# Two transformer blocks with routed experts: tokens and sums are turned before their norms, one more place for weights, a branch moved

## What is computed

```python
def reference(x, mem, ...):
    z = rms_norm(x, norm_mix) @ w_in          # u, v, q, k, val: tokens of x
    ... gated unit, differential attention, x = x + mixed
    x = x + memory_attention(rms_norm(x, norm_xq), rms_norm(mem, norm_mem), ...)
    x = x + hierarchical_moe(rms_norm(x, norm_ffn), ...)   # silu(t @ gate[e]) * (t @ up[e]) @ down[e]
    x = rms_norm(x, norm_final)
    q, k, v = split(rms_norm_2(x, norm_mix_pre_2) @ attn_w_qkv_2)
    ... x = x + rms_norm_2(attention @ w_o, norm_mix_post_2)
    return x + rms_norm_2(square(relu(rms_norm_2(x, norm_ffn_pre_2) @ w_up_2)) @ w_down_2, norm_ffn_post_2)

def rms_norm(x, g): return x * rsqrt(mean(x * x) + 1e-6) * g
```

## Time and profile before

| | us |
|---|---|
| runs shown: median (lowest to highest) | 1015.07 (1014.17 to 1015.34) |
| the profiled execution's own time | 1013.95 |
| its span in the trace | 1012.7 |
| TensorE busy | 956.6 |
| VectorE busy | 441.1 |
| ScalarE busy | 360.3 |
| DMA: 289.66 MB, mean GB/s | 286 |

### The profile page before, as it was taken

How to read it: one execution, slowest core, us unless ns; L and a number is a source line. 1 busy time by engine, 2 the same in 40 slices (tenths; PEclk the granted TensorE clock), 3 DMA queues, 4 the chain that set the end, 5 groups by cost and what they waited for, 6 DMA issues and landing times.

```text
span 1012.7 us, 13539 instructions
## 1 busy us (share of the span) xinstructions
PE 956.6 (94%) x5353; PEld 653.8 (65%) x5353; DVE 441.1 (44%) x757; ACT 360.3 (36%) x593; POOL 26.2 (3%) x40
## 2 busy tenths in 40 slices
PE   6999989998999999999999999985999989999997
PEld 5979878985444444444444444332998879998886
DVE  5856555445232232222222222214564755555434
ACT  7635446433121121111111112114455544554332
POOL 1400000000000000000000000000000000000000
PEclk9989999998999999999999999999999989999999
DMA  9943443486899999999999999999645535555501
GB/s 319 361 146 126 167 164 134 161 316 264 311 430 421 429 428 426 427 429 428 429 428 430 428 428 428 428 428 362 212 156 165 167 107 164 180 192 172 205 1 42
DMA packets 72629, 289.66 MB, mean 286 GB/s; under 512 B 4993, under 2 KB 44545, under 8 KB 60546
## 3 DMA queue, kind: packets, MB, share of 16 engines
q1 hardware_dynamic: 72002, 288.79, 73.8%
q10 hardware_dynamic: 576, 0.17, 0.1%
HBM read 287.90 MB, written 1.05 MB: 285 GB/s over the span
## 4 chain that ended last, share of the span: by engine, by line
PE 79%; issue 6%; ACT 6%; DVE 5%; DMA 4%; POOL 1%; SPq 0%; ACTq 0%; DVEq 0%
PE bank L1519 21%; PE bank L433 11%; PE bank L434 11%; PE bank L435 11%; PE bank L1541 10%; PE bank L1493 4%; DMA ring<-in_w_up 3%; ACT w_high L494 3%; PE bank L1552 3%; DVE w_low L523 1%; DVE arena L2303 1%; PE bank L1530 1%; ACT hidden_high L2127 1%; PE bank L723 1%; PE bank L761 1%
## 5 line engine op out<-in xcount | busy, mean ns | idle before, releaser
L1519 PE MATMUL bank<-ring,arena 128*64 128x512 f32 x1024 | 228.7, 598 | 7.9 <-issue 7.1
L523 DVE TENSOR_TENSOR w_low<-ring,w_high 128x2048 fp32r<-128x2048 f32 x76 | 174.1, 2290 | 122.3 <-ACT w_high L494 122.3
L494 ACT ACTIVATE w_high<-ring 128x2048 fp32r<-128x2048 f32 x76 | 145.1, 1909 | 120.8 <-PE bank L435 120.7
L1519 PEld LDWEIGHTS bank<-ring,arena 128*64 128x64 f32 x1024 | 75.5, 137 | 140.9 <-issue 139.0
L1541 PE MATMUL bank<-ring,arena 128*64 128x512 f32 x512 | 116.9, 597 | 5.3 <-issue 5.3
L433 PE MATMUL bank<-xT_high,w_high 128*128 128x256 f32 x384 | 112.0, 292 | 2.6 <-DVE xT_low L532 1.8
L434 PE MATMUL bank<-xT_low,w_high 128*128 128x256 f32 x384 | 109.8, 286 | 0.0
L435 PE MATMUL bank<-xT_high,w_low 128*128 128x256 f32 x384 | 109.7, 286 | 0.0
L1644 DVE SCALAR_TENSOR_TENSOR y_low<-bank,arena,y_high 64x512 fp32r<-64x512 f32 x64 | 48.0, 750 | 139.3 <-ACT y_high L1584 138.8
L1584 ACT ACTIVATE y_high<-bank,arena 64x512 fp32r<-64x512 f32 x64 | 43.7, 683 | 135.3 <-PE bank L1541 134.9
L1571 ACT ACTIVATE arena<-bank 128x256 f32<-128x256 f32 x32 | 12.3, 385 | 191.1 <-PE bank L1519 191.1
(11 more groups left out here) (280 smaller groups left out, 1455.9 us busy)
## 6 DMA issues: line engine op xcount, KB each, us to landing
ring<-in_w_down SPq DMA_DIRECT2D x32, 2048.0 KB, 25.0
ring<-in_w_gate SPq DMA_DIRECT2D x31, 2048.0 KB, 21.3
ring<-in_w_up SPq DMA_DIRECT2D x31, 2048.0 KB, 25.8
ring<-in_w_up SPq DMA_DIRECT2D x16, 1024.0 KB, 5.6
ring<-in_w_down SPq DMA_DIRECT2D x16, 1024.0 KB, 5.0
ring<-in_attn_w_qkv SPq DMA_DIRECT2D x12, 1024.0 KB, 11.8
ring<-in_w_in SPq DMA_DIRECT2D x10, 1024.0 KB, 11.7
ring<-in_w_kv_mem SPq DMA_DIRECT2D x8, 1024.0 KB, 5.2
```

The lines of the kernel that those rows point to most:

```text
L494: SC.activation(parts[buffer[0][u]][0][:, :], lanes[n % len(lanes)], ACT.Copy).then_inc(*high.inc(u))
L523: DVE.tensor_tensor(p[1][:, :], lanes[n % len(lanes)], p[0][:, :].bitcast(F32), ALU.subtract).then_inc(*split.inc(u))
L1519: last = PE.matmul(GU[t * SLOTS:(t + 1) * SLOTS, 0:NGU], xs[:, k, :], wgu[:, :, k, t * (DE // JT):(t + 1) * (DE // JT)], start=k == 0, sto ...
```

## The change

- **Tokens raw.** x's rows are transposed as loaded. Square, mean and power of x follow beside products. The norm of each token is put on the products: a row of norms, made wide (`widen`), turned ("rh") and copied, multiplies the banks of u, q and k when VectorE evacuates them (`features_out`); v and val take it as a scale per partition. u's Gelu runs on the evacuated values. mem is loaded behind u0 and turned behind u1.
- **Sums raw.** The four banks of the experts' sums are copied as they are and transposed; the gain column is norm_mix_pre times norm_final, and the norms of q, k, v are put on their products as above ("r1"). The product with the row norm_final, its squares and the means follow behind. norm_final's row is loaded behind the last experts' weights.
- **Places.** `extra` is a tenth piece; `bc` lies in it. Expert 3's down weights use it, and the places of experts from 4 on move up by one (`places_of`), with new waits in `early_loads`. The second block's lanes and parts are set to match.
- **Branch.** The last pair's scatter stands behind the branch, with a signal of its own after the first 128 tokens.
- **Constant products.** `keep_busy`: 8 products of ones into bank 7 before x's transposes, 6 behind them.
- The scratch area for dynamic DMA is set to 2048 bytes.

```diff
-hT00 hT01 hT10 hT11 +v.0 +v.1 -v.0 -v.1 u0@2 memT00@6 memT01@7 memT10@0 memT11@1 u1@3 q0@4 sguw@5 k0@2 +O0@6 +O1@7
+hT00 hT01 hT10 hT11 +v.0 +v.1 -v.0 -v.1 u0@2 rh@6 u1@3 memT00@6 memT01@7 memT10@0 memT11@1 q0@4 sguw@5 k0@2 +O0@6 +O1@7
...
-    bc = nc.alloc_sbuf_tensor("gain_rows", [P, 1024], F32)
...
+    extra = nc.alloc_sbuf_tensor("extra_piece", [P, PIECE], F32)
+    bc = extra[:, 0:1024]
...
-    lanes1, parts1 = pieces(*LANE_SLOTS), weight_parts("w1", slot_at(3))
+    lanes1, parts1 = pieces(*LANE_SLOTS), weight_parts("w1", slot_at(3), slot_at(3) + 2 * TILE)
...
-    lanes2, parts2 = pieces(3, 4, 5, 6), weight_parts("w2", slot_at(0))
+    lanes2, parts2 = pieces(3, 4, 5, 6), weight_parts("w2", slot_at(1), slot_at(0))
...
+    def keep_busy(bank, n):
+
+        for _ in range(n):
+            PE.matmul(bank[:, 0:P], ones[:, :], ones[:, :], start=True, stop=True, skip_group_check=True)
...
-        for u in order1[0:2]:
+        for u in order1[0:3]:
             load_first(u)
         for h in range(NH):
             SP.dma_start(memX[:, h, :], a["mem"][0, h * P:(h + 1) * P, :]).then_inc(*loads.inc(f"mem{h}"))
-        for u in order1[2:4]:
-            load_first(u)
+        load_first(order1[3])
...
-        load_row("norm_final", a["norm_final"].rearrange("(l n) -> l n", l=1))
+        SP.dma_start(gains[:, G_FINAL, :], a["norm_final_column"]).then_inc(*loads.inc("gain_final"))
...
+        PE.wait_ge(*consts.at("ones"))
+        keep_busy(banks[7], 8)
         PE.wait_ge(*consts.at("ident"))
-        turn(bank1, "hT", [(rows_v.at(f"h{h}"), rows_s.at(f"h{h}")) for h in range(NH)])
+        turn(bank1, "hT", [(loads.after(f"x{h}", 1),) for h in range(NH)], src=X)
+        keep_busy(banks[7], 6)
...
+        bank = open_bank(bank1, "rh")
+        for h in range(NH):
+            PE.wait_ge(*norm_wide.at(f"h{h}"))
+            last = PE.transpose(bank[:, h * P:(h + 1) * P], wide_h[:, h * P:(h + 1) * P], ident[:, :])
+        last.then_inc(*turned.inc("rh"))
+        f("u1", hT)
...
+        def u_gelus(u, t):
+            SC.wait_ge(*bank1.freed(u))
+            SC.activation(t, t, ACT.Gelu).then_inc(*u_gelu.inc(u))
...
-        for h in range(NH):
-            SC.wait_ge(*loads.after(f"x{h}", 1))
-            square_sum(X[:, h, :], XN[:, h, :], f"h{h}", stat("h", h))
-        for h in range(NH):
-            scale_half("h", h, XN, X)
...
+        high("u1")
         for h in range(NH):
             scale_half("mem", h, memX, memX)
-        SC.wait_ge(*early1.at("v.1"))
-        evacuate(bank1, "v.0", v[:, 0, :], func=ACT.Gelu)
-        SC.wait_ge(*unit1.at("v.1"))
-        evacuate(bank1, "v.1", v[:, 1, :], func=ACT.Gelu)
-        high("u1")
-        feature_out("u0", flat(uT[:, 0:2, :]), func=ACT.Gelu)
+        for h, whole in ((0, early1), (1, unit1)):
...
+            SC.wait_ge(*whole.at("v.1"))
+            SC.wait_ge(*rstd.at(f"h{h}"))
+            evacuate(bank1, f"v.{h}", v[:, h, :], stat("h", h), ACT.Gelu)
         high("q0")
+        SC.wait_ge(*turned.at("rh"))
+        evacuate_part(bank1, "rh", row_h)
+        u_gelus("u0", flat(uT[:, 0:2, :]))
+        high("k0")
+        u_gelus("u1", flat(uT[:, 2:4, :]))
         SC.wait_ge(*loads.after("gain_mem", 1))
+        turned_highs(bank1, "memT", 1, memT[0], G_MEM)
...
+        def features_out(u, dst, scale):
+
+            DVE.wait_ge(*unit1.at(u))
+            DVE.wait_ge(*bank1.freed("rh"))
+            DVE.scalar_tensor_tensor(out=dst, in0=banks[bank1.bank[u]][:, :].rearrange("p (n t) -> p n t", t=S),
+                                     scalar=scale, in1=row_h.rearrange("p (n t) -> p n t", n=1).to_broadcast([P, 2, S]),
+                                     op0=ALU.mult, op1=ALU.mult).then_inc(*bank1.inc(u))
...
+        features_out("u0", uT[:, 0:2, :], 1.0)
...
         low("q0")
-        turned_lows(bank1, "memT", 0, memT, G_MEM)
+        features_out("u1", uT[:, 2:4, :], 1.0)
+        low("k0")
...
+        features_out("q0", qT[:, 0:2, :], float(DQK) ** -0.5)
+        low("val.0")
+        features_out("k0", kT[:, 0:2, :], 1.0)
...
+        features_out("q1", qT[:, 2:4, :], float(DQK) ** -0.5)
         low("km0")
+        features_out("k1", kT[:, 2:4, :], 1.0)
...
-    def gate_up(q, n, w, buffer, e, chunks_=range(KC)):
+    def gate_up(q, n, gate, up, buffer, e, chunks_=range(KC)):
         xs = XTE[buffer][:, :, e * SLOTS:(e + 1) * SLOTS]
-        wgu = ring[:, w * PIECE:(w + 2) * PIECE].rearrange("p (m c n) -> p m c n", m=2, c=KC)
+        wgu = ring[:, :].rearrange("p (s c n) -> p s c n", s=RING, c=KC)[:, gate:up + 1:up - gate, :, :]
...
+        if mark:
+            last.then_inc(mark, 1)
...
+    def expert_loads(q, n, n0):
+
+        gate, up, dn = places_of(n0)
+        SP.wait_ge(*q.at("gate_up", n - 2))
+        if up < gate + 2:
+            load_piece(gate, expert_of(w_gate, n), place_sem[gate])
+            load_piece(up, expert_of(w_up, n), place_sem[up])
+        else:
+            load_piece(up, expert_of(w_up, n), place_sem[up])
+            load_piece(gate, expert_of(w_gate, n), place_sem[gate])
+        SP.wait_ge(*q.at("down", n - 2))
+        load_piece(dn, expert_of(w_down, n), place_sem[dn])
+
+    EXTRA = RING
+
+    def places_of(n):
+
+
+        if n < 4:
+            w = (6 + 3 * n) % RING
+            return w, w + 1, EXTRA if n == 3 else w + 2
+        w = (5 + 3 * n) % RING
+        return (1, w, 0) if w + 1 == RING else (w, w + 1, w + 2)
...
+        elif n == 3:
+            for part in range(4):
+                if part < 3:
+                    SP.wait_ge(quarters, part + 1)
+                else:
+                    SP.wait_ge(*q.at("gate_up", 1))
                 o = slice(part * PIECE // 4, (part + 1) * PIECE // 4)
-                SP.dma_start(ring[:, (w + i) * PIECE:(w + i + 1) * PIECE][:, o], src[3][:, o]).then_inc(slot_sem[w + i], 16)
-        SP.wait_ge(*q.at("down", 1))
-        SP.dma_start(ring[:, (w + 2) * PIECE:(w + 3) * PIECE], w_down[3]).then_inc(slot_sem[w + 2], 16)
+                SP.dma_start(piece(gate)[:, o], w_gate[n][:, o]).then_inc(place_sem[gate], 16)
+                SP.dma_start(piece(up)[:, o], w_up[n][:, o]).then_inc(place_sem[up], 16)
+            SP.wait_ge(*vgain.at(1))
+            load_piece(dn, w_down[n], place_sem[dn])
...
+            first, second = ((gate, w_gate), (up, w_up)) if gate < up < gate + 2 else ((up, w_up), (gate, w_gate))
+            SP.wait_ge(*q.at("down", n - 3))
+            load_piece(first[0], first[1][n], place_sem[first[0]])
+            SP.wait_ge(*q.at("gate_up", n - 2))
+            load_piece(second[0], second[1][n], place_sem[second[0]])
+            load_piece(dn, w_down[n], place_sem[dn])
...
-    for u in order2[0:6]:
+    for u in order2[0:4]:
         load_second(u)
     SP.wait_ge(*q.at("gate_up", NE - 1))
+    for u in order2[4:6]:
+        load_second(u)
+    load_row("norm_final", a["norm_final"].rearrange("(l n) -> l n", l=1))
...
-    scatter(q, NE, NE, LAST % 3, 0, False)
-    scatter(q, NE, NE, LAST % 3, 1, True)
...
+    tokens0_scattered = nc.alloc_semaphore("tokens0_scattered")
+    scatter(q, NE, NE, LAST % 3, 0, False, tokens0_scattered)
+    scatter(q, NE, NE, LAST % 3, 1, True)
...
-        turn(bank2, "pT", [(rows_v.at(f"p{h}"),) for h in range(NH)])
+                PE.wait_ge(*norm_wide.at(f"{r}{h}"))
+                last = PE.transpose(bank[:, h * P:(h + 1) * P], wide[r][:, h * P:(h + 1) * P], ident[:, :])
+            last.then_inc(*turned.inc(r))
+
+        for h in range(NH):
+            turn_sum("pT", h, XN, [bank2.freed(f"z{2 * h + j}") for j in range(2)], "pT")
...
+        turn_norms("r1")
...
+        def z_copy(b):
+            evacuate(bank2, f"z{b}", XN[:, b // 2, 512 * (b % 2):512 * (b % 2 + 1)])
...
-        part_squares("z", 0, ["z0", "z1"])
-        part_square("z", 1, 0, "z2")
-        z_squares(0)
-        part_square("z", 1, 1, "z3")
-        z_squares(1)
-        turned_highs(bank2, "pT", 0, xT2[0], G_PRE2)
-        turned_highs(bank2, "pT", 1, xT2[0], G_PRE2)
+        z_copy(3)
+        SC.wait_ge(*z_gained.at("columns"))
+        for c4 in range(2):
+            for h in range(NH):
+                turned_highs(bank2, "pT", h, xT2[0], G_PRE2, groups=(c4,))
+        for h in range(NH):
+            SC.wait_ge(*bank2.freed(f"z{2 * h}"))
+            SC.wait_ge(*bank2.freed(f"z{2 * h + 1}"))
+            z_squares("zr", h, XN, arena[3], small[:, 16 + 2 * h:17 + 2 * h])
...
+        SC.wait_ge(*z_gained.at(0))
+        z_squares("z", 0, X, arena[4], small[:, 20:21])
+        high("q0")
+        SC.wait_ge(*z_gained.at(1))
+        z_squares("z", 1, X, arena[4], small[:, 21:22])
...
+        norm_row("r1")
...
+        def z_gain(h):
+            for b in (2 * h, 2 * h + 1):
+                DVE.wait_ge(*bank2.freed(f"z{b}"))
+            DVE.tensor_tensor(X[:, h, :], XN[:, h, :], bc[:, :], ALU.mult).then_inc(*z_gained.inc(h))
...
+        DVE.wait_ge(*loads.after("gain_final", 1))
```

(24 more changed lines are left out.)

276 lines of the change are left out of this document (147 added, 129 removed).

## The result

| | before | changed |
|---|---|---|
| median, lowest to highest, us | 1015.21, 1014.17 to 1016.53 | 1006.61, 1005.58 to 1008.21 |
| the profiled execution, us | 1013.95 | 1006.05 |
| its span | 1012.7 | 1004.8 |

The ratio is 0.991 (95% interval 0.9893 to 0.9926): faster by 8.6 us, forecast 8.5. The sum was right; its first term had the wrong sign in the traces, and the two others were off by about 1 us each. I read the start of the same products in both traces; the stretches add up to each trace's last product.

What follows compares the result with a forecast made beforehand. TensorE works almost everywhere, so only its gaps can be won; the DMA's stream sets the expert stage's end. Gains 1.7 + 2.8 + 4.0 = 8.5 take the profiled 1013.95 to 1005.4; median forecast 1006.6, range 1001.5 to 1012.0.

Steps and rivals of the forecast that it cites:

- first term: First block to its first scores: turning tokens raw gains 1.7 us, bounds 0 and 2.9.
- the two stalls I priced: First block: TensorE loses 0.8 us waiting for q0; k0's evacuation queues behind low val.0, first scores near 48.9.
- The term of 1.7: First block to its first scores: gain from tokens turned raw, 1.7 us, bounds 0 and 2.9.
- size 2.8: Expert stage: the extra piece for weights lets loads start earlier, a lead of 2.8 us, bounds 2.0 and 4.1.
- the dry second at 272: Expert stage: the DMA moved nothing from 272 to 273 before; with the earlier issues it never runs dry there.
- 5.0 for 4.0: Between experts and second block: raw sums and the moved branch gain 4.0 us, bounds 2.0 and 6.4.
- the 6.4: Between the blocks: first product at 704.1 instead of 710.54, saving 6.4 us before deductions for clock and branch.
- The deduction of 2.1 for the clock: Between the blocks: half clock on products loses up to 3.4 us, 1.6 if in the scatter; 2.1 taken.
- The branch's 0.3: Branch moved ahead of the last scatter, under a 3.0 us wait: cost between 0 and 0.9, 0.3 taken.
- The rival of a fetch behind the branch: Branch ahead of the last scatter: the jump outlasts its wait, scatter up to 2.4 us late, 1009.0; chance 0.07.
- cost 0: Feature units' evacuations moved from ScalarE to VectorE: 8.2 us of VectorE beside a full TensorE, cost 0.
- The slow side: Rival: moved evacuations delay the lows behind them, 3.0 us for each of twelve, 18 if half, 1024.6; chance 0.05.

Runs made afterwards that it cites:

- a1: The changed kernel without its two groups of constant products (8 and 6) at the start: median 1007.72 us, ratio 0.992 to the kernel before.
- a3: The changed kernel with the last pair's scatter ahead of the branch over the spill code again, sums still raw: 1008.92 us, ratio 0.9935.
- b1: The kernel before with k3 moved to bank 6, a2 to 7 and a3 to 1 in the second attention: 1013.37 us, ratio 0.9974.
- c1: The changed kernel with nine constant products behind the last down product, ahead of the branch, in TensorE's wait for the last y: 1008.77 us, ratio 0.9921.
- c2: The changed kernel with six constant products in TensorE's wait for the chosen experts and three ahead of the first gather: 1003.80 us, ratio 0.9874.
- d0: The changed kernel itself, unaltered, measured again: 1005.74 us, ratio 0.9897 to the kernel before.
- e3: The kernel with waits filled before the experts and at the second attention's end, but loads of experts 3 to 6 at before's events: 1002.76 us, ratio 0.9865.
- c3: The changed kernel with five constant products ahead of turning the second attention's sums and six behind it: 1004.32 us, ratio 0.9877.
- e2: The kernel with waits filled before the experts and at the second attention's end, the gating's second-half products moved behind val.1: 1003.27 us, ratio 0.9867.

## Why the prediction was right, and where it was not

**First block: wrong.** The step to the first product held: 10.05 against 9.75, v.0's first high at 8.55 against 8.4; the 1.35 us from there were 1.5. The first constant products took 3.78 us for the 2 I gave them, being at half rate; that cost nothing, since without them (a1) the transposes start at 4.82 instead of 4.79. Of the two stalls I priced, low q0's was 1.31 for 0.8 (0.42 in a3), first scores 49.33 for 48.9. What failed is that the sum ends at the first scores: it has no term from there to the experts. Two things took 2.1 us. One is the same queue of VectorE I had watched at q0, further on: k1's evacuation stands behind low km0, and the fifth scores wait for it, 1.56 us instead of the 0.88 in the kernel before (0.7 us):
```profile
87.97 0.49 PE L691 MATMUL bank<-arena 64*128 64x128 f32 x4 [1.56 <-DVE arena L1134]
```
The other is the clock, which I followed only between the blocks. Most of the gating and the products behind it run at half:
```profile
62.00:66.00 4.00, 4.00 (x11) 2.91 (x12) 2.83 (x2) 0.46 (x1) 0.00 (x0) 0.50 0.10 16
66.00:70.00 4.00, 4.00 (x11) 3.04 (x11) 1.98 (x3) 0.80 (x2) 0.00 (x0) 0.50 0.60 246
```
for 10.2 us here and 6.8 before (62 to 69), 1.5 us more. The comparison with b1 above gives the same split, 0.6 and 1.5. In seven other executions with the new first block it is 6.8, and 3.4 more at 131 to 137, 10.2 again; c1 and c2 have 10.2 and 3.4. The first gather came at 243.64 and 243.60 in two executions of before's first block, at 243.87 to 244.65 in the eight of the new one with 10.2 us at half. The term of 1.7 was -0.95 in the pair of traces and -0.3 to -1.0 over these executions, below its lower bound of 0. But the third execution of before's block, b1, had its first gather at 247.38, by its half-rate start (1.8 us) and 3.4 us more at half clock. Against it the new block gains 2.7 to 3.5 us. So the failed term is shown for the traces compared; what it is on average needs more executions of the kernel before. b1 has 3.4 us at 135 to 140 as well, so the second fall isn't the new block's alone; why it came in the other two not at all is open.

**Experts' stream: mechanism right, size 2.8 for about 2.** Every issue came in the predicted order and spacing, the dry second at 272 went, waits of 4.7 us for the 5.1 forecast. That last agreement is partly luck. The waits were 7.2 us in a1 and 3.6 in d0 with the new events. The changed kernel's clock was at half for 3.4 us at 667 to 671, and its last wait for weights, 1.4 us near 683 (the 1.39 of the earlier trace rows), is missing. In all 14 traces one goes with the other: where the clock falls at some point from 664 to 672 us (eight) that wait is absent, where it doesn't (six) it is there, 1.4 us. TensorE works longer and the weights catch up, so a fall there costs next to nothing. The waits fell by 3.2 us and the stretch to the last gate-up by only 1.9 (446.5 to 444.6), since the other 1.3 went into that slower work. The one pair of traces can't give the lead more closely: the stage varies by 3.3 us.

**Between the blocks: right in kind, 5.0 for 4.0.** Of the 6.4, clock and branch took less. The deduction of 2.1 for the clock mixed a fall on v0.0 (3.4) with one in the scatter (1.6); with raw sums and the scatter behind the branch it began between 0.7 us ahead of the scatter's start and 1.3 behind it, in all executions but e3, which had none. It lasted 3.4 us (6.8 in c3) and was over before the first product of v0.0 each time. In the changed kernel's trace it cost 1.0. Copies and highs took 0.4 more than I had given them. The branch's 0.3 was 0 in this trace, 0.8 in three others and 0.4 in one, 0.3 on average over the nine: its size was right, but not for a reason I knew, and neither did I know that the other place costs 2.9 (a3). The rival of a fetch behind the branch had the stall at the right place and its price, at most 2.4, too high: what stands out of the 3.0 us of waiting is 0 to 0.8. The Trainium skill (Runtime: NRT & Kernel Launch, section Instruction fetch mechanics) says that a taken branch to code outside the pages at hand stalls for a fetch; TensorE's 2.87 us of "issue" in a3 fit that, though no row shows the fetch itself, and ScalarE and VectorE went on within 0.03 us at the same place.

**Moved evacuations: "cost 0" was -1.** No lows waited in the second attention but k0's, 0.73 us at 722.33, and two transposes were added, 0.2; against it the 1.83 at v1.0 went. The slow side was nowhere near. (The prediction counts twelve moved units; with u0 and u1 there are fourteen.) The rest, 1.0 us behind 814, is the clock: 3.4 us at half there instead of 6.8, and that differs between executions (v1.0 to the end takes 229.9 to 230.7 us in the four traces with 6.8 us at half between 777 and 830, 228.9 to 229.1 in the six with 3.4).

So 8.5 came out of 1.9 - 2.8 + 1.9 + 5.0 + 0.9 + 1.0 = 7.9 in the traces, with errors of -2.6, -0.9, +1.0 and +1.9. The total was closer than its parts deserve: that is luck. No experiment turns the tokens or the sums raw by themselves; what that is worth is read from the waits that are gone in the pair of traces.

## What to carry over

A branch costs where no wait covers it: put it under a wait that is longer than the branch in several traces (3.0 us was enough in five executions of nine), fill that wait with nothing else, and look for it as "issue" between two groups that depend on nothing new. When an operation is added to a rotation of banks, list who now follows whom; one place more won 1.8 us here. Short waits ahead of dense work can be filled with products that nobody reads (here 4.0 us for two places), but compare stages over several traces, since the clock and the DMA alone move a stage by 1 to 3 us.

## What was unexpected of the hardware

- TensorE was at half rate at its start with 1.00 in the clock's column: 128x512 products of 0.63 us for 0.39, sixteen transposes in 3.64 us for 2.20. The durations tell it, the column does not.
- The branch over code that isn't run took TensorE 2.87 us, with the reading of its flag 3.2 to 3.8 us.
- In the eight traces of 14 in which the clock fell for 3.4 us near 668, a wait for weights of 1.4 us behind it was gone.
- The clock was at half for 6.8 to 10.2 us while TensorE had no gap (60 to 71 us), and full products beside the small ones did not mend it (e2). The Trainium skill (TensorE: Matmul & The Clock Gate, section The HAM clock gate) has half rate as the default that activity releases; the start, c2 and c3 agree, the gating's rows, 4.00 us busy of 4.00 at 0.50, do not.
- The expert stage, bound by the DMA over most of its length, took 451.3 to 454.7 us in different executions with its code unchanged.
